# Asking for the next block's input tiles ahead of the weight splits, in the first phase of an encoder layer

## The reference

```
xn   = rms_norm(x, g_attn_pre)              # (2048, 1024)
proj = xn @ w_in                            # (1024, 2304)
qa, ka, va, qb, kb, vb = split(proj, [512, 640, 768, 1280, 1792])
qa, ka get a per-head rms norm and a rotary turn
```

## Time and profile before

| what | value |
|---|---|
| median of 3 runs | 3778.66 (3775.55 to 3782.97) |
| the profiled execution's own time | 3778.64 |
| its span | 3776.8 |
| PE busy | 3566.6 (94%) |
| PEld busy | 3032.1 (80%) |
| DVE busy | 2232.6 (59%) |
| ACT busy | 1555.0 (41%) |
| POOL busy | 1667.0 (44%) |
| mean granted TensorE clock | 0.969 of full speed |

### The profile page before, as it was taken

The page is one execution under the profiler, slowest core; times in us unless marked ns, Lnnn a source line. Parts: engine busy times, 40 slices in busy tenths (PEclk is TensorE's granted clock), DMA queues, the critical chain, the costliest instruction groups (busy, mean ns, idle before and its releaser), DMA issues.

```text
span 3776.8 us, 55262 instructions
## 1 busy us (share of the span) xinstructions
PE 3566.6 (94%) x18812; PEld 3032.1 (80%) x18812; DVE 2232.6 (59%) x3807; ACT 1555.0 (41%) x3166; POOL 1667.0 (44%) x1180
## 2 busy tenths in 40 slices
PE   7999979999999999999699998999989999899997
PEld 6777768888888899999478887788877888778885
DVE  5334448888888878778344455444464434643443
ACT  2212248888888777777322114221142211411112
POOL 4454410000000133434356664666656666566663
PEclk9999989999999999999799999999999999999998
DMA  4444421111002044333223334333343333433331
GB/s 154 150 151 141 139 96 50 50 50 50 17 17 50 24 87 93 63 78 104 83 89 106 101 95 140 123 106 104 97 140 123 106 101 96 144 112 95 102 100 56
DMA packets 264712, 356.84 MB, mean 94 GB/s; under 512 B 172500, under 2 KB 191388, under 8 KB 258492
## 3 DMA queue, kind: packets, MB, share of 16 engines
q1 hardware_dynamic: 255164, 340.42, 30.1%
q10 hardware_dynamic: 9344, 13.73, 1.0%
HBM read 310.81 MB, written 55.74 MB: 97 GB/s over the span
## 4 chain that ended last, share of the span: by engine, by line
PE 46%; DVE 5%; ACT 1%; issue 1%; DVEq 0%
PE feed_bank L1505 45%; DVE feed_res L1766 2%; DVE feed_total L1763 1%; PE feed_bank L1496 1%; DVE feed_xT L1748 1%; ACT feed_xT L1634 0%; DVE feed_fs L1836 0%; DVE feed_xn L1739 0%; ACT feed_junk L1611 0%; DVE feed_total L1841 0%; DVE feed_rec L1730 0%; DVE feed_ms L1727 0%; ACT feed_junk L1625 0%; ACT feed_rstd L1601 0%; DVE feed_total L1810 0%
## 5 line engine op out<-in xcount | busy, mean ns | idle before, releaser
L1472 POOL TENSOR_TENSOR feed_w_split<-feed_w_raw,feed_w_split 128x1024 fp32r<-128x1024 f32 x328 | 839.8, 2560 | 27.4
L1505 PE MATMUL feed_bank<-feed_xT,feed_w_split 128*128 128x512 f32 x3072 | 705.4, 391 | 7.9 <-DVE feed_total L1841 5.4
L1505 PE MATMUL feed_bank<-feed_w_split,feed_fT 128*128 128x512 f32 x3072 | 700.6, 389 | 0.0
L1470 POOL TENSOR_SCALAR feed_w_split<-feed_w_raw 128x1024 fp32r<-128x1024 f32 x328 | 348.2, 1062 | 770.2 <-issue 748.9
L1505 PEld LDWEIGHTS feed_bank<-feed_xT,feed_w_split 128*128 128x128 f32 x3072 | 579.1, 189 | 129.8 <-issue 6.6
L1505 PEld LDWEIGHTS feed_bank<-feed_w_split,feed_fT 128*128 128x128 f32 x3072 | 576.2, 188 | 119.4
L356 PE MATMUL proj_bank<-proj_w_split,proj_xT 128*128 128x512 f32 (+1 forms) x1920 | 416.4, 379 | 37.1 <-ACT proj_sq L416 18.0
L356 PEld LDWEIGHTS proj_bank<-proj_w_split,proj_xT 128*128 128x128 f32 x1920 | 344.1, 197 | 105.6 <-ACT proj_st L424 20.6
L1662 ACT ACTIVATE feed_rl<-feed_bank 128x512 f32<-128x512 f32 x128 | 76.6, 598 | 802.3 <-PE feed_bank L1505 802.3
L882 DVE TENSOR_TENSOR mixa_pT<-mixa_turned,mixa_pT 128x512 fp32r<-128x512 f32 x512 | 348.2, 685 | 81.7 <-ACT mixa_pT L828 78.1
L1505 PE MATMUL feed_bank<-feed_w_split,feed_xT 128*128 128x512 f32 x1536 | 369.0, 401 | 4.9 <-DVE feed_xT L1748 4.9
(11 more groups left out here) (173 smaller groups left out, 4530.1 us busy)
## 6 DMA issues: line engine op xcount, KB each, us to landing
feed_w_raw<-w_tail_dram SPq DMA_DIRECT2D x328, 512.0 KB, 3.6
proj_w_raw<-w_in_dram SPq DMA_DIRECT2D x39, 1024.0 KB, 5.0
scr_table<-scr_bias SPq DMA_DIRECT2D x8, 1520.0 KB, 8.5
proj_x_t<-x_dram SPq DMA_DIRECT2D x20, 512.0 KB, 6.7
mixa_q_in<-scr_qA SPq DMA_DIRECT2D x36, 256.0 KB, 3.4
mixb_q_in<-scr_qB SPq DMA_DIRECT2D x18, 512.0 KB, 5.7
mixb_k_in<-scr_kB SPq DMA_DIRECT2D x18, 512.0 KB, 7.8
feed_res<-x_dram SPq DMA_DIRECT2D x16, 512.0 KB, 5.9
```

The lines of the kernel that those rows point to most:

```text
L1470: pool.tensor_scalar(w_sp[0][:, half, :], w_raw[:, slot, :], 1.0, 0.0, ALU.mult, ALU.add).then_inc(w_hi, 1)
L1472: pool.tensor_tensor(w_sp[1][:, half, :], w_raw[:, slot, :], w_sp[0][:, half, :].bitcast(F32), ALU.subtract).then_inc(w_lo, 1)
L1505: mm = pe.matmul(dst, lhs, rhs, start=start, stop=stop)
```

## The change

SP's requests for the four input tiles of the next block move. They are no longer sent with i = 0, 2, 4 and 6 behind the wait for `w_lo` and the weight load, but with i = 0 (tiles 0 and 1), i = 1 (tile 2) and i = 2 (tile 3), in front of that wait and of the weight load. The waits for `xn_done` go with them. Nothing else moves.

```diff
+    X_AT = {0: (0, 1), 1: (2,), 2: (3,)}
...
                     for i in range(NCH):
                         c = NCH * u + i
+                        for t in X_AT.get(i, ()):
+                            sp.wait_ge(xn_done, b * TT + t + 1)
+                            sp.dma_start(x_t[:, t, :], x[bass.ds((b + 1) * BT + t * P, P), :]).then_inc(x_in[t], 16)
                         sp.wait_ge(w_lo, it * (2 * NCH) + c + NRAW + 1)
                         load_w(c + NRAW)
-                        if i % 2 == 0 and i // 2 < TT:
-                            t = i // 2
-                            sp.wait_ge(xn_done, b * TT + t + 1)
-                            sp.dma_start(x_t[:, t, :], x[bass.ds((b + 1) * BT + t * P, P), :]).then_inc(x_in[t], 16)
                         if i in BIAS_AT:
```

## The result

The changed kernel took 3754.26 us in the median of 4 runs (3752.48 to 3757.13), the kernel before 3778.1 beside it (3775.55 to 3782.97): a ratio of 0.9936, 95% interval 0.992 to 0.9952. Run again in another session, it took 3751.05 against 3777.96, ratio 0.9931 (0.9917 to 0.9945). The forecast was 3751.6 with a range of 3744 to 3763. The profiled execution's span is 3751.4 us, against 3776.8: 25.4 less.

What follows compares the result with a forecast made beforehand. PE was taken to bound the first phase, with its savings saving the whole kernel. The gap's 18.9 us plus the clock's 8.1 gave 27.0, taken from 3778.64 for 3751.6 us, range 3744 to 3763.

Steps and rivals of the forecast that it cites:

- What bounds the phase: First phase: PE sets its end, busy 108.10 of block 0's 116.71 us; whatever PE is saved, the whole kernel is saved.
- The gap: Group 0 to 1: PE's wait on eviction L416, held up by ScalarE's wait for tile 1, goes; 18.9 us over four blocks.
- The clock behind it: Chunks 2 and 3: full clock returns once PE no longer idles before them; 8.1 us over four blocks.
- Rival 1: Chunks 2 and 3: the gap goes but the clock's part doesn't come back; 3759.7 us, chance 0.20.
- The prediction's check: Chunks 2 and 3: lengths less the clock's cost give 22.3, 22.4, 22.3 and 22.1 us, the same work at full speed.
- Chunk 5's draw: Clock over chunk 5, now costing 6.2 us, is drawn anew: 6.2 us better to 5.4 us worse.
- The gap ahead of chunk 5, and 3 to 4: Groups 2 to 3 and 3 to 4: L424's waits hang on PE's position and stay, near 16 us.
- Weights behind the tiles: Chunk 3's weights, requested at about 19.8 behind two tiles in block 0, still land in time; cost nothing.
- Rival 3: Splits of chunks 3, 4 and 5: weights land late behind the tiles, making the kernel slower; 3791.6 us, chance 0.03.
- The fetch: Block's start: requests coming together may delay an instruction fetch; PE's gap there 3.0 us; taken as 0, 3 us kept for range.
- Rivals 2 and 4: 2: wait passed to next boundary, about 3778.6 us, chance 0.07; 4: request not early enough, about 3765, chance 0.04.

Runs made afterwards that it cites:

- e1: Only the request for tile 1 moved to the front of the block, against the kernel before: 3748.3 us, ratio 0.992.
- e2: Only the requests for tiles 0, 2 and 3 moved as in the change, tile 1 left late, against the kernel before: 3777.6 us, ratio 0.9993.
- e3: No request moved; tile 1's square and norm moved from i = 0 to i = 2, against the kernel before: 3752.26 us, ratio 0.9919.
- e6: Only tile 1's request moved to the front of the block, run again beside the changed kernel: 3752.08 us, ratio 0.993 to the kernel before.
- e7: Changed kernel with squares and norms of tiles 2 and 3 moved from i = 4, 6 to 5, 7: 3724.85 us, ratio 0.9864 to the kernel before.
- e9: No request moved; squares and norms of tiles 1, 2, 3 moved to i = 2, 5, 7, against the kernel before: 3729.61 us, ratio 0.9873.
- e10: Changed kernel with squares and norms of tiles 1, 2, 3 at i = 2, 5, 7: 3728.04 us, ratio 0.9869 to the kernel before.
- e8: Kernel before, requests unmoved, with squares and norms of tiles 2 and 3 moved to i = 5 and 7: 3752.45 us, ratio 0.9938.
- e4: Tile 1 requested at i = 2, behind the wait for chunk 2's split but ahead of the weight load, against the kernel before: 3760.61 us, ratio 0.9951.

## Why the prediction was right

- *What bounds the phase.* PE did, and all that it was spared came off the kernel: 25.1 us in the phase, 25.4 in the span.
- *The gap.* Forecast 18.9 us gone; no wait on L416 is left. e1, e2 and e3 show that it was tile 1 alone, and the place in the order where it was waited for.
- *The clock behind it.* Forecast 8.1, measured 7.3. The mechanism held: in the eight traces without this gap (the change twice, e1, e3, e6, e7, e9, e10) all 32 stretches of chunks 2 and 3 take 22.5 us, and in the three with the whole gap (before, e2, e8) all 12 take longer. Rival 1, that this part would not come back, is out. The term was too large because length times the missing clock counts a us at half speed as half a us lost. The trace before shows less. Two stretches within chunk 2, at either clock:

```profile
411.00:416.80 5.80, 5.80 (x27) 5.80 (x28) 5.29 (x10) 4.22 (x11) 2.64 (x2) 0.50 0.01 3
62.50:70.00 7.50, 7.50 (x65) 7.50 (x64) 7.20 (x7) 2.51 (x12) 6.35 (x2) 1.00 0.13 27
```

  That is 4.7 matmuls per us against 8.7, a factor of 1.9 and not 2, so by an estimate from these rows a us at half speed costs 0.46. It makes 7.5 of the 8.1; the rest is within the rounding of the clock column. The prediction's check, 22.1 to 22.4 us for the same work, shows the error: the full-speed length is 22.5.
- *Chunk 5's draw.* Forecast as a term of 0 between 6.2 better and 5.4 worse; it came out at 0.1 better, and that it came out near nothing was luck. The second trace of the same kernel has chunk 5 at about 11.2, 12.6, 11.2 and 12.6 us, the first at 11.2, 12.7, 14.0 and 12.8. The Trainium skill (TensorE: Matmul & The Clock Gate, Part 1) says that the moment of a change isn't tied to the kernel's own time and varies from run to run; these two traces agree.
- *The gap ahead of chunk 5, and 3 to 4.* Said to stay as they hang on PE's position: L424's waits are 16.0 after 16.1. That holds for this change, but "all of it hangs on PE's position" left out ScalarE's order: e7 removes both gaps by the same reordering.
- *Weights behind the tiles.* Forecast a request at about 19.8 and no cost. It went out at 20.02 and landed 6.7 us later, behind the two tiles, where about 40 would have been needed to cost anything. The only wait of GpSimd for a weight chunk in the phase is the one of 10.5 us at the start that was there before. Rival 3 has no support. One reading was off without consequence: the prediction gave two issues 0.34 us each, but the first of them took 5.6 us of the 8.70; SP then still waited for VectorE's norm before the second.
- *The loop's turn.* The fetch was taken as 0 with 3 us kept for the range: the gap without a releaser is 3.04 us before and 2.97 after.
- *Rivals 2 and 4.* No new wait took the gap's place, and the request was early enough: ScalarE was through with tile 1's square some 13 us before the first eviction.
- *What the sum didn't hold.* Chunk 0 of block 0 took 1.35 us more, at a clock column of 1.00 in both. The eight transposes just before it take 1.94 us, where those inside the loop take 1.03, and the stretch from 31 to 34 us holds 14 matmuls before and 8 after:

```profile
31.00:34.00 3.00, 3.00 (x14) 2.42 (x13) 2.09 (x5) 1.41 (x4) 0.00 (x0) 1.00 0.01 3
```

```profile
31.00:34.00 3.00, 3.00 (x8) 2.33 (x8) 2.10 (x5) 2.43 (x6) 0.00 (x0) 1.00 0.43 169
```

  So PE was at half speed there, for longer after than before. The column doesn't show it: the first clock record of the trace is at 31.3 us before and at 34.2 after, and without a record it reads 1.00. By the estimate above the 2.9 us between them cost 2.9 x 0.46 = 1.3, which is the 1.35. Over the twelve traces this chunk takes between 11.7 and 13.1 us. With the late requests it takes up to 12.5 (e8) and with the early ones as little as 11.7 (e10), so the 1.35 are not shown to be the change's; the trace of the kernel before happens to be at the short end.

## What to carry to other kernels

In an engine's fixed order, a wait for something that nobody needs soon must stand behind the work that others wait for. Look for an engine that is idle most of the time and still late: ScalarE was busy for 41% here and held PE up at three of five group changes. Moving the late transfer and moving the waiting instruction cure the same gap, and the second one also reaches the places where the thing waited for isn't a transfer. And price a gap of PE with the half speed behind it: here 7.3 us on top of 18.9.

## What the runs showed of the hardware

Half speed never followed PE's shortest gaps and always followed the longest; between 1.8 and 3.3 us it came in some cases and not in others. The first four rows count the kernel before, the change and e1 to e6, with four blocks each, and e8 for the long gaps. The last three are the loop's turn, once in each of the twelve traces.

| PE's gap | followed by half speed |
|---|---|
| 1.5 to 1.7 us (group 3 to 4) | 0 of 32 |
| 1.8 to 2.1 us (e4, group 0 to 1) | 2 of 4 |
| 2.4 us (group 2 to 3) | 23 of 32 |
| 4.2 to 4.6 us (group 0 to 1: before, e2, e8) | 12 of 12 |
| 1.5 and 1.7 us (loop's turn: e2, e1) | 0 of 2 |
| 2.2 to 3.3 us (loop's turn) | 5 of 9 |
| 4.7 us (loop's turn: e6) | 1 of 1 |

In the middle the length doesn't order the cases. Two rows of the loop's turn, in e3 and in the change's second trace, show a shorter gap with half speed behind it and a longer one without:

```profile
254.06 14.05 PE L356 MATMUL proj_bank<-proj_w_split,proj_xT 128*128 128x512 f32 x48 [2.86 <-issue]
```

```profile
253.63 11.19 PE L356 MATMUL proj_bank<-proj_w_split,proj_xT 128*128 128x512 f32 x48 [3.27 <-issue]
```

Ahead of the 2.4 us gap PE also runs the small bias matmul, for 0.80 us; whether the drops behind it have to do with that is not shown. The count is by the length of the chunks behind the gap, from start to start: 11.0 or 11.1 us at full speed for one, 22.5 for chunks 2 and 3, and 1.2 to 2.9 us more otherwise. Within a kernel the blocks differ without a difference in the code.
